# Two modulation tiles behind each projection tile, convolution sums in SBUF, and 16 taps ahead of each low part

## What is computed

```
mod = silu(c) @ ada_w + ada_b                 # 6 x 1024: sh1, sc1, g1, sh2, sc2, g2
xn  = rmsnorm(x, norm1_g) * (1 + sc1) + sh1
q, k, v, ca, cg = split(xn @ w_in)            # 512 columns each
a   = silu(group_norm(causal_dwconv31(ca * sigmoid(cg)), 8 groups))
y   = concat(attention(rmsnorm(q), rmsnorm(k), v, rel_bias), a) @ w_out   # 8 heads x 64
x   = x + g1 * y
xn2 = rmsnorm(x, norm2_g) * (1 + sc2) + sh2
u, g = split(causal_dwconv3(xn2 @ w_up))      # 2 x 2816
x   = x + g2 * ((silu(g) * u) @ w_down)
```

## Time and profile before

| | |
|---|---|
| runs | 378.49, 378.70, 379.08 us, median 378.7 |
| the profiled execution | spans 375.6 us from its first to its last instruction; no other time is recorded for it, so the median of the runs is 3.1 above its span |
| granted TensorE clock, mean | 0.981 |
| busy, share of the span | TensorE 95%, weight load 79%, VectorE 72%, ScalarE 47%, GpSimd 7% |
| DMA | 79.51 MB, mean 212 GB/s |

### The profile page before, as it was taken

The page is one execution under the profiler, slowest core; times in us unless marked ns, Lnnn a source line. Parts: engine busy times, 40 slices in busy tenths (PEclk is TensorE's granted clock), DMA queues, the critical chain, the costliest instruction groups (busy, mean ns, idle before and its releaser), DMA issues.

```text
span 375.6 us, 6095 instructions
## 1 busy us (share of the span) xinstructions
PE 355.7 (95%) x2410; PEld 297.2 (79%) x2410; DVE 269.4 (72%) x489; ACT 176.4 (47%) x255; POOL 26.3 (7%) x67
## 2 busy tenths in 40 slices
PE   7979899999399989999999999999999999999995
PEld 6668878997055437777799899998989899999984
DVE  2654699999995538756888776768586667658665
ACT  4354624244004455837674553635544644636430
POOL 5381000000000100002300000000000000000000
PEclk9999999999789799999999999999999999999999
DMA  7999978698482686551074545544645555410003
GB/s 281 427 422 421 420 291 310 263 383 330 200 336 113 218 311 255 191 202 58 0 275 175 219 148 195 215 166 181 225 126 211 185 166 209 172 57 0 3 0 112
DMA packets 12797, 79.51 MB, mean 212 GB/s; under 512 B 1368, under 2 KB 2784, under 8 KB 3552
## 3 DMA queue, kind: packets, MB, share of 16 engines
q1 hardware_dynamic: 12560, 78.97, 55.5%
q10 hardware_dynamic: 144, 0.13, 0.1%
q0 software_dynamic: 64, 0.01, 0.0%
HBM read 78.05 MB, written 1.06 MB: 211 GB/s over the span
## 4 chain that ended last, share of the span: by engine, by line
PE 72%; DVE 19%; DMA 4%; ACT 2%; issue 1%; POOL 0%; ACTq 0%; DVEq 0%; POOLq 0%
PE bank L882 20%; PE bank L883 19%; PE bank L884 19%; DVE bank L650 10%; DVE w_lo L558 4%; DMA raw<-in_stream 3%; PE bank L904 3%; PE bank L1143 2%; PE bank L929 2%; PE bank L1163 1%; PE bank L940 1%; DMA xt<-in_x_t 1%; PE bank L1153 1%; PE bank L1065 1%; DVE act_hi L812 1%
## 5 line engine op out<-in xcount | busy, mean ns | idle before, releaser
L882 PE MATMUL bank<-act_hi,w_hi 128*128 128x256 f32 x480 | 138.1, 288 | 3.7 <-DVE glu L659 1.5
L883 PE MATMUL bank<-act_lo,w_hi 128*128 128x256 f32 x480 | 135.7, 283 | 0.0
L884 PE MATMUL bank<-act_hi,w_lo 128*128 128x256 f32 x480 | 135.6, 283 | 0.0
L558 DVE TENSOR_TENSOR w_lo<-raw,w_hi 128x2048 fp32r<-128x2048 f32 x45 | 103.5, 2301 | 27.6 <-ACT w_hi L348 27.6
L882 PEld LDWEIGHTS bank<-act_hi,w_hi 128*128 128x128 f32 x480 | 91.8, 191 | 12.8 <-issue 8.5
L348 ACT ACTIVATE w_hi<-raw 128x2048 fp32r<-128x2048 f32 x45 | 85.8, 1908 | 14.2 <-DMA raw<-in_stream 13.2
L883 PEld LDWEIGHTS bank<-act_lo,w_hi 128*128 128x128 f32 x480 | 91.9, 191 | 0.4
L884 PEld LDWEIGHTS bank<-act_hi,w_lo 128*128 128x128 f32 x480 | 91.9, 191 | 0.0
L650 DVE SCALAR_TENSOR_TENSOR bank<-glu,cols,bank 128x256 f32<-128x256 f32 x116 | 46.1, 478 | 0.0
L518 ACT ACTIVATE bias<-bank,cols 128x256 f32<-128x256 f32 x44 | 22.2, 555 | 35.8 <-PE bank L884 35.8
L882 PE MATMUL bank<-w_hi,hid_hi 128*128 128x512 f32 x88 | 34.8, 396 | 0.0
(11 more groups left out here) (164 smaller groups left out, 353.1 us busy)
## 6 DMA issues: line engine op xcount, KB each, us to landing
raw<-in_stream SPq DMA_DIRECT2D x71, 1024.0 KB, 5.9
xt<-in_x_t SPq DMA_DIRECT2D x2, 512.0 KB, 4.6
bias<-toeplitz_rows SPq DMA_DIRECT2D x1, 1024.0 KB, 10.8
xr<-in_x_rows SPq DMA_DIRECT2D x1, 1024.0 KB, 8.8
out<-xmod SPq DMA_DIRECT2D x3, 256.0 KB, 2.1
gates_b<-in_ada_b_gates SPq DMA_DIRECT2D x1, 256.0 KB, 8.6
cols<-in_cols SPq DMA_DIRECT2D x1, 185.0 KB, 5.4
out<-xmod SPq DMA_DIRECT2D x1, 128.0 KB, 1.9
```

The source lines that it names most:

```text
L558: nc.vector.tensor_tensor(w_lo[:, m % PARTS, :], slot(*SPLIT[m]), w_hi[:, m % PARTS, :].bitcast(f32), ALU.subtract).then_inc(lo_done, 1)
L882: nc.tensor.matmul(o, sh, mh, start=first, stop=False)
L883: nc.tensor.matmul(o, sh, ml, start=False, stop=False)
L884: return nc.tensor.matmul(o, sl, mh, start=False, stop=last)
```

## The change

Two modulation tiles follow each projection tile from conv 2 to q/k 3, twelve in all where there were seven; one follows v 0, one stands between the halves of v 1, and one each is left for heads 0 and 1. The order of the stream changes with it. The conv sums lie in `conv` in SBUF from the first tap on, so the wait of tile 16 for the taps falls away. VectorE works 16 taps per tile, and ahead of the low part. After the statistics it works 4 and 4 taps, normalises q/k 0 and 1, adds the gate rows, and then works the last 4 taps. The second half of v 1 now stands ahead of the spreads of q/k 2 and 3. The identity transposes that ended the modulation groups are gone; VectorE waits for `ada_used` itself.

```diff
-ADA_AFTER = {("conv", 2): 1, ("conv", 3): 1, ("qk", 0): 1, ("qk", 1): 1, ("qk", 2): 1, ("qk", 3): 2}
-ADA_AT_HEAD = (2, 2, 1)
+ADA_AFTER = {("conv", 2): 2, ("conv", 3): 2, ("qk", 0): 2, ("qk", 1): 2, ("qk", 2): 2, ("qk", 3): 2}
+ADA_AT_HEAD = (1, 1)
+TAPS_A_TILE = 16
...
-            return bank[CONV_BANK[j // 2]][:, (j % 2) * SEQ:(j % 2) * SEQ + SEQ]
+            return conv[:, j, :]
...
-                dve.wait_ge(mod_done, 2)
+                dve.wait_ge(ada_used, 3 * KT)
                 nc.vector.tensor_copy(mod_rows[:, :], bank[7][:, :]).then_inc(mod_rows_ready, 1)
...
-                        to = conv_sum(j) if i < CONV_TAPS - 1 else conv[:, j, :]
-                        nc.vector.scalar_tensor_tensor(to, glu[:, j, i:i + SEQ], w, conv_sum(j),
+                        nc.vector.scalar_tensor_tensor(conv_sum(j), glu[:, j, i:i + SEQ], w, conv_sum(j),
                                                        ALU.mult, ALU.add).then_inc(tap, 1)
...
             for m in range(SP_AT["v", 0] + 1):
                 if m >= 1:
                     after(m - 1)
+                if m >= 2:
+                    taps(TAPS_A_TILE)
                 if 1 <= m <= SP_AT["v", 1] - 2:
                     split_lo(m + 2)
-                if 2 <= m:
-                    taps(14)
...
             taps(4)
             dve.wait_ge(qk_turned, 1)
             nc.vector.tensor_copy(qk_rstd[:, :], bank[6][0:16, SEQ:2 * SEQ]).then_inc(qk_rs, 1)
-            taps(len(TAPS))
+            taps(4)
             qk_normalise(0)
             qk_normalise(1)
 
-            dve.wait_ge(mod_done, 1)
+            dve.wait_ge(ada_used, 2 * KT)
             dve.wait_ge(gates_b_ready, 16)
             nc.vector.tensor_tensor(gates_b[:, :], bank[2][:, :], gates_b[:, :], ALU.add).then_inc(mod_rows_ready, 1)
+            taps(len(TAPS))
             qk_normalise(2)
             qk_normalise(3)
...
-                if n == 2 * KT:
-                    pe.wait_ge(tap, PAIR_TAPS[0])
...
             v_half(0, 0)
             qk_squares(CT - 1)
             v_half(0, 1).then_inc(w_used, 1)
+            late_ada(1)
             qk_turn()
-            if ada_at[0] == 2 * KT:
-                ada_end(2)
-            late_ada(3)
+            v_half(1, 0)
+            late_ada(1)
             qk_spread(0)
             qk_spread(1)
-            v_half(1, 0)
-            late_ada(1)
+            v_half(1, 1).then_inc(w_used, 1)
             qk_spread(2)
             qk_spread(3)
-            v_half(1, 1).then_inc(w_used, 1)
...
                 if h < len(ADA_AT_HEAD):
                     late_ada(ADA_AT_HEAD[h])
-                    if h == len(ADA_AT_HEAD) - 1:
-                        ada_end(3)
                 head_values(h)
```

More of the change, by code:

```diff
@@ L70 @@
 PAIR_TAPS = (len(TAPS) // 2, len(TAPS))
-CONV_BANK = (7, 3)
 def bucket_ranges():
@@ L175, in hymba_layer @@
             sem(s) for s in ("silu_c_ready", "xsq_left", "xsq_right", "ssq_ready", "rms_ready"))
-        mod_done, mod_rows_ready, mod_cols_ready = sem("mod_done"), sem("mod_rows_ready"), sem("mod_cols_ready")
+        mod_rows_ready, mod_cols_ready = sem("mod_rows_ready"), sem("mod_cols_ready")
         mod_cols_read = sem("mod_cols_read")
@@ L906, in ada @@
                 last.then_inc(ada_used, 1)
-            def ada_end(groups):
-                pe.wait_ge(ada_used, groups * KT)
-                nc.tensor.transpose(bank[7 if groups == 2 else 5][:, SEQ:SEQ + P], ident[:, :], ident[:, :]).then_inc(mod_done, 1)
             def turn_mod_rows(to):
@@ L1011, in _, with late_ada @@
             ada_at = [KT]
+            def late_ada(n):
+                for _ in range(n):
+                    ada(ada_at[0], 2 if ada_at[0] < 2 * KT else 7)
+                    ada_at[0] += 1
             def later_ada(after):
-                for _ in range(ADA_AFTER.get(after, 0)):
-                    ada(ada_at[0], 2)
-                    ada_at[0] += 1
+                late_ada(ADA_AFTER.get(after, 0))
             for j in range(FIRST, CT):
```

## The result

The changed kernel takes 381.0 us (median of 20 runs, 379.07 to 387.34), the kernel before 378.6 (20 runs). The ratio is 1.0065, 95% interval 1.0044 to 1.0087: slower by about 2.4 us. The forecast was 376.9, faster by 1.8, range 373.0 to 379.4. The time lies outside the range and on the other side. Where some runs of a kernel took over 1.5% longer than its fastest, its ratio leaves them out and its median doesn't, so the two can differ by a little.

A forecast was written before the change was run, and what follows sets the result against it. VectorE was taken as the bound up to 99.95 us, then TensorE's order. Scores 2.6 later less 4.4 saved in the heads gave -1.8 us, span 373.8, plus 3.1 around it: 376.9, range 373.0 to 379.4.

The forecast's parts named there:

- The tap: One conv tap on VectorE with its sums in SBUF: 0.39 us, bounds 0.33 and 0.50.
- The stream and the low parts: Conv tile 3 lands at 42.6 and becomes VectorE's wait, first tap at 47.1; q/k low parts reach TensorE in time.
- The statistics: Reciprocal of the q/k statistics on VectorE done at 104.9; TensorE, ready at 99.3, idle for 5.9 us.
- The low clock behind the idle stretch: TensorE's slowed clock after idling for the statistics, in v 1's first half: 1.8 us lost, of at most 2.9.
- part 3: From the q/k statistics to the first scores: scores at 119.4 against 116.84, 2.6 us late, bounds 0.7 and 3.6.
- Part 4: Heads 0 to 2, with fewer modulation tiles: saves 1.6, 2.2 and 0.6, sum 4.4 us, bounds 3.6 and 4.9.
- The heads give less: Rival: thinly loaded heads 0 to 2 keep TensorE at 1.2 GHz, taking back 2 us; 378.9 us, 20 in 100.
- Cheaper and dearer taps: Rivals on SBUF taps: 0.33 us each, 369.1, 6 in 100; or 0.50 to 0.66, 389.0 to about 407, 8 in 100.

The follow-up runs named there:

- e3: Changed kernel with 9, 9 and 12 extra identity transposes in heads 0, 1 and 2: 377.9 us, ratio 0.9991 to the kernel before.
- e12: Changed kernel with 18, 18 and 24 extra identity transposes in heads 0, 1 and 2: 382.0 us, ratio 1.0115 to the kernel before.
- e4: Changed kernel with 60 extra identity transposes ahead of the statistics' transpose and 9, 9 and 12 in heads 0 to 2: 377.8 us, ratio 0.998.
- e10: Kernel before with three modulation tiles moved from heads 0 to 2 to ahead of the scores, same work: 386.7 us, ratio 1.0211.
- e5: Changed kernel with the modulation tiles put back where they were, 2, 2 and 1 in heads 0 to 2: 377.9 us, ratio 0.999.
- e1: Kernel before with one edit, the conv sums in SBUF from the first tap on: 378.4 us, ratio 0.9985.
- e2: Changed kernel with 60 extra identity transposes ahead of the transpose of the q/k statistics: 380.85 us, ratio 1.0023 to the kernel before.
- e9: Changed kernel with 14 taps a tile, the rest respread, 32 extra transposes ahead of the statistics and 9, 9, 12 in heads: 375.5 us, ratio 0.994.

## Why the prediction was wrong

**What held.** *The tap.* I took 0.39 us, measured 0.395. Of the two rules of the Trainium skill, the one of "VectorE: DVE Perf Modes" (TRN2 errata) would by my estimate have given 0.33 and the one of "Vector Engine (DVE) Microarchitecture Reference" (points that are easy to get wrong) 0.66; the runs show neither. *The stream and the low parts.* Conv tile 3 became the wait, as said, but its high part started 0.9 later than I had it (43.50 instead of 42.6; the seven other runs with this order of the stream have 42.5 to 43.5), so the taps began at 48.0 instead of 47.1. No q/k tile was late: TensorE has no wait between 49 and 99 us. *The statistics.* Reciprocal at 105.94 for 104.9, with that 0.9 as the cause. TensorE was done at 99.2 for 99.3. So it idled 7.1 instead of 5.9.

**What was mis-sized.** *The low clock behind the idle stretch*, in part 3: "I take 1.8, between none and all". It was nearly all: 5.4 for the half of v 1 instead of 2.86, 2.5 lost. With the 0.9 of the transfer, the scores came 3.98 late instead of 2.6, beyond my bound of 3.6. It was no bad draw: e3 and e12 are the same program up to the heads, and the same half took 5.2 and 5.3 us in them. e4 with the clock held had the scores at 117.85.

**What failed.** Part 4, the heads: "I save 1.6 ... I save 2.2 ... Sum 4.4", and "from head 3 on nothing changes in order, ... so the difference is carried to the end". That sum prices all that stays in the heads at the speed it had before. The order doesn't change, but the speed does. I had priced the tiles as work on the path and had read in the earlier trace rows that they ran partly at 1.2 GHz, and took them for sufferers of the low clock. In the kernel before, the clock was up again behind each pair of them (scores of heads 2 and 3 in 0.92 us, at 126.44 and 133.78). With them gone the low stretch grew from pieces to 14 us and reached into heads 3 to 5. The saving up to the values of head 2 was 2.6 instead of 4.4, and 4.35 were lost behind them. e3, e10 and e12 show it from three sides: extra work in the heads wins 3.1, three tiles taken out of the heads of the kernel before cost 8.1 in all, and a second dose of extra work wins nothing and costs itself. The tiles put back (e5) win 3.1 as well, but more than half of that lies ahead of the heads in its profile.

**The rivals.** *The heads give less* was the right mechanism, with a chance of 20 in 100 and a price of 2 us. The profiled execution, 2.1 us slower than the median, shows 6.1 (4.4 forecast saved, 1.7 lost on balance). Between the medians 4.2 us are missing (1.8 forecast gained, 2.4 lost) for this and the mis-sized stretch ahead of the scores together. Cheaper and dearer taps are both excluded by e1. At the full clock the forecast's terms are about right, as e4's profiled execution shows: scores at 117.85 for 117.6, and from there to the values of head 2 19.06 us, of which 2.3 are fill in heads 0 and 1, so by my estimate 16.8 for the forecast 17.5. What the forecast lacked is that the change itself takes this clock away.

**Open.** How much load in the heads is enough was tried at two doses only, and no run says why one execution of a program keeps its clock where the next doesn't. Whether the last normalisations, exposed for 0.97 us ahead of the scores, are worth their old place wasn't tried by itself; e3 and e5 keep them so and lose nothing against before.

## What to carry to other kernels

In this kernel small matmuls between waits left TensorE "busy" for 12.1 of 14.0 us at a clock of 0.52. So independent matmuls among such steps may be more than work on the path: price their removal a second time, with the steps behind them at their low-clock durations. When such work is moved away, try the place once with an equal amount of identity transposes in it; if that is as fast as the empty place, or faster, leave the work there. Where the runs of one program differ by percents, list time against granted clock first.

## What the runs showed of the hardware that I had not expected

The same instructions in another order, e10, cost 8.1 us (2.1%); in its profiled execution two thirds of the loss (6.3 of 9.9 us) lie in the heads, out of which 3 us of work had been taken. At the two levels of the clock, 2.4 and 1.2 GHz, scores took 0.92 and 1.65 us, three transposes 0.55 and 0.90, a gate spread 1.12 and 2.07, and half of v 2.86 and 5.4. The wait in head 2 follows: from the start of the gate spread to the values it takes 3.97 us in the changed kernel and 3.02 in e3, and the 0.95 between them is what the slow spread takes more. Identity transposes could keep the clock up: it was 1.00 in 100 to 108 us of e2, with 60 of them, and 1.00 in 125 to 155 us of e3, with 30 in the heads; the same 30 left it at 0.94 in e9. And one execution of the changed kernel took 379.1, another 387.3, with no other difference on record than a granted clock of 0.973 and 0.945.
